# Gate projections of a recurrence spread over all of its heads, one per eight levels

## What is computed

```python
z = h @ w_in                                    # q_pre, f_pre, i_in, g_pre, 1024 columns each
f = lb + (1.0 - lb) * sigmoid(f_pre);  k = 1.0 - f;  q = silu(q_pre);  v = i_in
...
a = einsum('bhtd,bhsd,bhtsd->bhts', qc, kc, decay)      # within a chunk
o_intra = einsum('bhts,bhse->bhte', a, vc)
...
o = o * rsqrt(mean(o * o, axis=-1) + NORM_EPS)
o = o * out_norm * silu(g_pre)                  # the gate
return o @ w_out
```

## Time and profile before

| what | value |
|---|---|
| median of 3 runs | 3044.89 us (3042.92 to 3047.72) |
| profiled execution, its own time | 3045.04 us |
| its span | 3043.1 us |
| mean granted TensorE clock | 0.991 |
| TensorE matmul busy | 2986.4 us (98%) |
| VectorE, GpSimd, ScalarE busy | 2372.9, 1323.3, 1200.4 us |
| the recurrence | 1602.57 to 1758.85 us from the span's start |

### The profile page before, as it was taken

One profiled execution on the slowest core, in us unless ns is written; L12 is line 12 of the kernel. 1 busy time (PEld: TensorE's weight loads), 2 busy tenths in 40 slices (PEclk: granted clock), 3 DMA queues, 4 the chain that ended last, 5 costly groups with the idle time before them and its releaser, 6 DMA issues.

```text
span 3043.1 us, 43968 instructions
## 1 busy us (share of the span) xinstructions
PE 2986.4 (98%) x16132; PEld 2639.7 (87%) x16132; DVE 2372.9 (78%) x4437; ACT 1200.4 (39%) x1878; POOL 1323.3 (43%) x749
## 2 busy tenths in 40 slices
PE   8999999999999999999999999999999999999998
PEld 7668999999998888888788878999999997888887
DVE  7437899888977888888356647999888968888888
ACT  5434333444433333333435543334444433333333
POOL 4213465444434544343446523565444434444442
PEclk9999999999999999999999899999999999999999
DMA  4203367999999999998221022468999999999996
GB/s 146 68 28 104 113 200 268 344 371 360 376 367 376 351 372 356 357 353 325 92 95 49 22 77 84 150 189 305 361 370 363 373 364 364 366 347 361 354 351 255
DMA packets 345861, 800.83 MB, mean 263 GB/s; under 512 B 27952, under 2 KB 192048, under 8 KB 345392
## 3 DMA queue, kind: packets, MB, share of 16 engines
q1 hardware_dynamic: 271776, 529.49, 49.9%
q0 software_dynamic: 73728, 268.47, 23.3%
q10 hardware_dynamic: 144, 0.07, 0.0%
HBM read 695.15 MB, written 102.76 MB: 262 GB/s over the span
## 4 chain that ended last, share of the span: by engine, by line
PE 91%; DVE 4%; DMA 3%; issue 1%; ACT 1%; SPq 0%; POOL 0%; DVEq 0%; ACTq 0%
PE PS L1496 28%; PE PS L1498 27%; PE PS L1497 27%; PE PS L1675 3%; DMA arena<-acts_dram 2%; PE PS L1746 1%; PE PS L1652 1%; DMA gates_dram<-arena 1%; PE PS L1630 1%; PE PS L1613 1%; PE PS L1612 0%; PE PS L1553 0%; DVE arena L1375 0%; PE PS L1620 0%; PE PS L1799 0%
## 5 line engine op out<-in xcount | busy, mean ns | idle before, releaser
L1496 PE MATMUL PS<-x_hi,w_hi 128*128 128x384 f32 (+1 forms) x2616 | 926.4, 354 | 9.5 <-DVE arena L1401 3.3
L634 ACT ACTIVATE w_hi<-w_raw 128x1024 fp32r<-128x1024 f32 x609 | 643.1, 1057 | 674.2 <-PE PS L1498 657.3
L1498 PE MATMUL PS<-x_hi,w_lo 128*128 128x384 f32 (+1 forms) x2616 | 907.7, 347 | 0.0
L1497 PE MATMUL PS<-x_lo,w_hi 128*128 128x384 f32 (+1 forms) x2616 | 906.0, 346 | 0.0
L571 POOL DMA_INDIRECT arena<-in_v_t,arena x256 | 451.7, 1764 | 598.0 <-DVE resid L1274 548.6
L1496 PE MATMUL PS<-w_hi,x_hi 128*128 128x512 f32 x1744 | 680.7, 390 | 7.3 <-DVE x_lo L1291 7.3
L1497 PE MATMUL PS<-w_lo,x_hi 128*128 128x512 f32 x1744 | 679.4, 390 | 0.0
L1498 PE MATMUL PS<-w_hi,x_lo 128*128 128x512 f32 x1744 | 679.4, 390 | 0.0
L560 POOL TENSOR_TENSOR w_lo<-w_raw,w_hi 128x1024 fp32r<-128x1024 f32 x169 | 421.0, 2495 | 539.3 <-ACT w_hi L634 539.1
L1251 DVE TENSOR_TENSOR w_lo<-w_raw,w_hi 128x1024 fp32r<-128x1024 f32 x440 | 538.1, 1223 | 107.7 <-ACT w_hi L634 107.5
L571 POOL DMA_INDIRECT arena<-in_u_rows,arena x256 | 381.0, 1488 | 487.2 <-DVE arena L1258 433.9
(11 more groups left out here) (186 smaller groups left out, 2390.1 us busy)
## 6 DMA issues: line engine op xcount, KB each, us to landing
w_raw<-in_u_t SPq DMA_DIRECT2D x256, 512.0 KB, 6.8
w_raw<-in_v_t SPq DMA_DIRECT2D x256, 512.0 KB, 6.7
acts_dram<-arena SPq DMA_DIRECT2D x256, 192.0 KB, 7.3
gates_dram<-arena SPq DMA_DIRECT2D x24, 2048.0 KB, 15.9
arena<-gates_dram SPq DMA_DIRECT2D x64, 768.0 KB, 7.6
arena<-acts_dram SPq DMA_DIRECT2D x256, 192.0 KB, 7.2
w_raw<-in_hg_t SPq DMA_DIRECT2D x40, 512.0 KB, 3.2
w_raw<-in_pq_t SPq DMA_DIRECT2D x32, 512.0 KB, 3.3
```

Source lines behind the costliest of these rows:

```text
L634: act.activation(w_hi[:, slot, :], w_raw[:, slot, :], ACT.Copy).then_inc(hi_ready, 1)
L1496: pe.matmul(ps, wh, xh, start=start, stop=False)
L1497: pe.matmul(ps, wh, xl, start=False, stop=False)
L1498: return pe.matmul(ps, wl, xh, start=False, stop=stop)
```

## The change

The 56 parts are filled in behind steps 4 to 59 instead of 4 to 45: eight parts per eight levels, in the pattern 2, 1, 2, 1, 1, 1, 0, 0 from level 4 on, instead of two behind each of four levels in six. `gate_finished` is now level 5 of every head instead of every sixth level. GpSimd's low parts of the weight tiles move with it: they stand behind step 16, 24, and so on to 56, the eighth one behind the loop. Since the last gate now reads its input in heads 6 and 7, the high parts of the first three heads, which overwrite that input, stand in levels 0, 2 and 4 of head 7 on ScalarE and wait for a new semaphore (`gate_room`) that TensorE raises behind parts 0, 1 and 2 of the last gate; the low parts stand in levels 1, 3 and 5.

```diff
--- before.py
+++ after.py
@@ -149,13 +149,13 @@
 
 
     n = 8 * h + p
-    return 2 if 4 <= n < 6 * HEADS - 2 and (n - 4) % 6 < 4 else 0
+    return (2, 1, 2, 1, 1, 1, 0, 0)[(n - 4) % 8] if 4 <= n < 8 * HEADS - 4 else 0
 
 
 def gate_finished(n):
 
 
-    return n // 6 if n % 6 == 5 and n // 6 < HEADS else None
+    return n // 8 if n % 8 == 5 else None
 
 
 def recurrence():
@@ -610,9 +610,9 @@
                 take_diff(n)
                 if n in (6, 9, 11):
                     lows(BASE["hg_g"] + n // 3, BASE["hg_g"] + n // 3 + 1) if n < 11 else                         lows(BASE["hg_g"] + RING, BASE["hg_g"] + RING + 1)
-                elif n >= 14 and n % 6 == 2 and (n - 8) // 6 < HEADS:
-                    lows(BASE["hg_g"] + RING + (n - 8) // 6, BASE["hg_g"] + RING + (n - 8) // 6 + 1)
-            lows(BASE["hg_out"] + RING, BASE["u1"] + FIRST_GATHER)
+                elif n >= 16 and n % 8 == 0:
+                    lows(BASE["hg_g"] + RING + n // 8 - 1, BASE["hg_g"] + RING + n // 8)
+            lows(BASE["hg_out"] + RING - 1, BASE["u1"] + FIRST_GATHER)
             gathers(1)
 
 
@@ -899,6 +899,8 @@
 
             def gated_high(h):
                 act.wait_ge(sem("gated"), h + 1)
+                if h < 3:
+                    act.wait_ge(sem("gate_room"), h + 1)
                 act.activation(x_hi[:, h, :], gq[:, h, :], ACT.Copy).then_inc(sem("gated_high"), 1)
 
             for n in range(2):
@@ -929,8 +931,8 @@
                         roots(0)
                     if (h, k) in ((6, 0), (6, 4), (6, 7), (7, 3)):
                         diagonal({(6, 0): 0, (6, 4): 1, (6, 7): 2, (7, 3): 3}[h, k], 0)
-                    if (h, k) in ((6, 4), (7, 1), (7, 5)):
-                        gated_high({(6, 4): 0, (7, 1): 1, (7, 5): 2}[h, k])
+                    if (h, k) in ((7, 0), (7, 2), (7, 4)):
+                        gated_high(k // 2)
 
             gated_high(3)
             roots(1)
@@ -1446,8 +1448,8 @@
                     head_rstd(0)
                 if (h, k) in ((6, 1), (6, 6), (7, 1), (7, 6)):
                     gated({(6, 1): 0, (6, 6): 1, (7, 1): 2, (7, 6): 3}[h, k])
-                if (h, k) in ((6, 4), (7, 0), (7, 4)):
-                    gated_low({(6, 4): 0, (7, 0): 1, (7, 4): 2}[h, k])
+                if (h, k) in ((7, 1), (7, 3), (7, 5)):
+                    gated_low(k // 2)
             mask_level(8 * HEADS - 2)
             mask_level(8 * HEADS - 1)
             gated_low(3)
@@ -1782,6 +1784,8 @@
                         begin(("hg_g", h))
                     mm = three(PSb(("hg_g", h)), w_hi[:, n % RING, w], w_lo[:, n % RING, w], x_hi[:, p, :],
                                x_lo[:, p, :], p == 0, p == KC - 1)
+                    if h == HEADS - 1 and p < 3:
+                        mm.then_inc(sem("gate_room"), 1)
                     if p == KC - 1:
                         end(mm, ("hg_g", h))
                 elif what == "project":
```

## The result

The changed kernel takes 3025.81 us (median of 4 runs, 3020.7 to 3027.97) against 3043.9 of the kernel before: a ratio of 0.9938, interval 0.9922 to 0.9953. By the medians that is 18.1 us less, where 13.2 were forecast: 3025.81 us for a forecast of 3032, near the lower end of the range of 3024 to 3041. Nearly all of it is in the stage that was cut into heads: 160.97 us before by the earlier trace rows, 143.04 now.

The account below looks back on a forecast made before the run. TensorE's matmuls, 91% of the chain, were taken to bound the kernel. Head terms -0.7, -6.8, -2.5, +0.6, -2.0 and -1.8 summed to -13.2 us, from 3045.04 to 3031.8, so 3032; range 3024 to 3041.

Parts of the forecast that it names:

- head 5: Head 5: tanh and split now ahead of the square roots hold up VectorE; +0.6 us, from -1 to +3.
- the rival of more gain: Heads 6 and 7 at their bounds and the piece behind at full clock: 3026 and below; chance 0.06.
- heads 6 and 7: Now with 8 and 2 gate parts, head 6 at full clock: -2.0 and -1.8 us; best bounds -3.5 and -3.7.
- Heads 2 and 3: Four gate parts fewer each; head 2 also loses the dear silu wait and low clock: -6.8 and -2.5 us.
- the slower rival: Each gate waits for its silu as in head 2, 2.8 us in each of seven heads: 3052; chance 0.05.
- Heads 1 and 4: They keep 8 parts, one now in level 7 before the next head: 0 us, +1 to -0.7 each.
- The rival of the clash: GpSimd's splits block VectorE at line 1443, 2.1 us in each of six heads, gain gone: 3045; chance 0.07.
- one of the signs that the prediction had set for being wrong: Wrong if line 1443 is long in each head and TensorE idles at each head boundary.
- The argument against this rival: Head 3 of the kernel before has just this split placement, and its 19.50 us come from its 12 parts.
- The 0.3 us for a start at the low clock: Head 6: 0.3 us added to 18.8 for starting at the low clock, making 19.1 us.
- The clock case, which had 0.17: Clock keeps falling: heads 6 and 7 gain nothing, head 5 costs its worst: 3038; chance 0.17.
- The waits for `gate_room`: Three added ScalarE waits for the last gate's parts: no cost, covered in head 7; 0.7 us without that cover.

Follow-up runs that it names:

- My direct test of it in the kernel before: Kernel before, with tanh, split and silu of gates 3 and 7 moved from level 7 to level 5, no gate part moved: ratio 1.0025.
- the last experiment: The clumped kernel with seven of the last gate's eight parts and the three waits for them left out: 3021.65 us, one time taken.
- the clumped kernel: Changed kernel with gate parts in the pattern 2, 2, 2, 2, 0, 0, 0, 0 from level 4 on: 3017.25 us, ratio 0.9921.
- the clumped kernel with the later scaling: The clumped kernel with VectorE's scaling of head 3 moved from level 6 to the end of level 7 of head 7: ratio 0.9946.

## Why the prediction was right

**The outline held.** TensorE sets the pace, and the stage is all of the difference: 17.9 us in the stage, 18.1 in the medians. So close an agreement is luck, since the rest of the span differs by up to 11 us from one profile to the next; the second measurement of the changed kernel has the ratio 0.9934, some 20 us.

**That the time lies in the range is in part luck too.** Heads 0, 5, 6 and 7 gained 6.9 us more than forecast, 4.6 of it in head 5, and heads 1 to 4 gained 2.3 less. Without these 2.3 the time would be some 3023.5 us and outside. It is also 0.2 us below the 3026 where the rival of more gain begins, but not by that rival's way: heads 6 and 7 stayed short of their bounds (3.1 and 2.3 for 3.5 and 3.7), and the piece behind took 4.70 us at the low clock.

**Heads 2 and 3**, the surest terms, came out at -6.2 and -1.9. The reason given, that the silu's place in level 7 costs a long wait and then the clock, is shown by the pattern two levels later: 1.58 us in each head, and 2.54 us or more per head with the clock. It is the slower rival's mechanism, which did not happen because level 5 costs 0.34 us there too. My direct test of it in the kernel before did not work, since it broke the distance between gate and tanh.

**Heads 1 and 4** were taken at 0 and are 0.5 and 0.6 longer, and heads 2 and 3 missed by the same 0.6. The rival of the clash is the cause, though not at its price: 0.84 us per head in heads 3 and 4 and 0.47 in head 1 instead of 2.1, since mostly the differences and not the split itself meet VectorE. The splits four levels later take it away, and head 4 is then 16.73 us, below the 16.99 of the kernel before. So one of the signs that the prediction had set for being wrong did come: line 1443 (now 1445) has a median of 1.56 us, and TensorE idles at the boundaries, but for 0.58 us and not for 2. The argument against this rival was a misreading. Head 3 of the kernel before had the clash already (1.20 and 1.57 us at 1672.16 and 1673.29); its parts ahead of the boundary covered it. The Trainium skill (SBUF — State Buffer, Who interferes with whom) says that the operation that comes second is blocked until the first is done; two rows agree with it, `gate_head` with 2.85 us beside a split of 2.35, and `gated_low` with 2.37 beside one of 2.37. Both end 0.54 to 0.55 us behind the split.

**Head 5 was wrong**: +0.6 forecast, -1 the lower bound, -4.0 measured. The step that failed is that tanh and split, put ahead of the square roots, would hold VectorE back by up to 1.63 us. The work did move, but into time in which ScalarE waited. Its timeline in the changed kernel, with the reciprocal on VectorE and the scale product on TensorE:

```profile
1695.37 0.59 ACT L850 ACTIVATE arena<-PS 128x512 f32<-128x512 f32 x1
...
1695.84 1.06 ACT L634 ACTIVATE w_hi<-w_raw 128x1024 fp32r<-128x1024 f32 x1
...
1697.41 0.41 ACT L877 ACTIVATE PS<-arena 128x256 f32<-128x256 f32 x1 [0.51 <-DVE arena L1355]
...
1699.17 1.28 ACT L889 ACT_TABLE_LOAD   x1
...
1700.71 0.25 DVE L1414 RECIPROCAL arena<-arena 128x16 f32<-128x16 f32 x1 [1.54 <-ACT arena L889]
...
1705.11 1.13 PE L1775 MATMUL PS<-arena,const 128*128 128x128 f32 x8 [1.74 <-ACT arena L897]
```

And in the kernel before, the same exponential on ScalarE as that at 1697.41, and VectorE's scaling just ahead of the reciprocal:

```profile
1704.00 0.41 ACT L877 ACTIVATE PS<-arena 128x256 f32<-128x256 f32 x1 [2.63 <-DVE arena L1353]
...
1705.50 0.69 DVE L1353 TENSOR_TENSOR arena<-arena,PS 128x512 f32<-128x512 f32 x1 [1.23 <-PE PS L1746]
```

ScalarE had 2.63 us of idle time there; tanh and split fit into it, and 0.51 us are left. VectorE waits 1.54 us for the roots, 0.8 more than the 0.75 us before the change, not 1.63; and the 1.23 us that it waited for TensorE just ahead of them are gone. In return the way from the roots to the scale product is shorter. By the windows TensorE's idle time in head 5 fell from 4.37 to 2.08 us, and its busy time from 19.34 to 17.59. From the experiments the 4.0 us divide so: the clock did not fall, 1.57 (the changed kernel against the same instructions with waste behind them); the split's place, 0.93 (22.17 against 21.24, both with the fall); the remaining 1.54 is the tanh's place and the parts that fill the hole, which were not told apart. GpSimd's split also ended ahead of the decay of the queries, which took 0.68 us instead of up to 2.84; that is within the second term and the third.

**Heads 6 and 7** gained 3.1 and 2.3 for 2.0 and 1.8. The direction was right and part of the reason too: waste on TensorE alone makes both heads shorter. But the reason was told too simply. The clock of the kernel before fell in the pause of head 5, not in head 6, came back near 1727, and fell once more at the end of head 6:

```profile
1732.00:1734.00 2.00, 1.26 (x10) 1.10 (x9) 1.74 (x5) 1.21 (x3) 0.86 (x2) 0.97 0.00 0
...
1734.00:1736.00 2.00, 2.00 (x10) 2.00 (x11) 1.98 (x4) 1.07 (x3) 0.64 (x2) 0.50 0.00 0
```

TensorE had idled 0.29 and 0.45 us there. In the changed kernel the clock did not fall in head 5, and head 6 has no idle time (busy 17.98 of 17.98 us). In the last experiment head 6 idles 2.5 us in all and keeps its clock, without cover; that is one profile, and how much of the gain is cover and how much the clock at its start stays open. The 0.3 us for a start at the low clock wasn't due. The clock case, which had 0.17, did not come in either profile of the changed kernel. The waits for `gate_room` cost nothing, as forecast: no idle time before line 904 of the changed kernel ends with TensorE.

**The Trainium skill** (TensorE: Matmul & The Clock Gate, A second HAM failure mode) would have had the clock go back and forth with frequent small pauses. In heads 2 to 4 of the changed kernel that is not so: they have 0.92 us of idle in two pieces each and stay at 1.00. Two places agree better with it: the fall at 1734 above, and the one behind 0.82 and 0.90 us in the clumped kernel with the later scaling.

## What to carry to other kernels

Here filler work was worth most where it stood ahead of the pause that it could fill, and it is judged by what it does to the waits and to the clock: 7.3 us of waste made the stage of the kernel before 4.1 us shorter, and 5.1 us of work left out gained nothing. When a projection is slotted into a pipeline, two distances count more than its spread: how far behind its last part the reader stands (with two steps instead of four ScalarE stood 6.2 us, and the two heads became 0.5 and 3.6 us longer), and what else the engine that frees its buffer has to do at that level (1.58 or 0.34 us in every round). Before an operation moved ahead of a wait is priced as a delay, look whether its engine was idle there.

## What the runs showed of the hardware

A pause of 1.7 us on TensorE, at the same place and with the same instructions around it, was followed by the low clock in one of four profiles and not in the other three; the one fall cost 1.57 us. Pauses of 1.09 to 1.11 us at this place, in four profiles of clumped kernels, had no fall, and those of 2.09, 2.47 and 2.67 us had it. Elsewhere shorter ones were enough: the clock fell behind idle times of 0.29 and 0.45 us in head 6 of the kernel before, and behind 0.82 and 0.90 us in head 7 of the clumped kernel with the later scaling. How long it then stayed low varied too. In head 2 of the kernel before, with gate parts, it was some 3 us, and from the end of head 5 on, with none, some 13. But with the pattern two levels later the first two falls, in heads 0 and 1, lasted some 7 and 10 us, with gate parts among the levels. The low clock of the windows is 0.50, that is 1.2 GHz of 2.4.
